# Order of the phases of sample attention in a decoder step: keys, values and what stands between them

## What is computed

```python
def nsa_heads(q, pos_q, comp, gather_sel, kv_win, pos_win, gates, slopes):
    o_c, p_c = cmp_attend(q, pos_q, comp, slopes)
    idx = select_blocks(jnp.sum(p_c, axis=3), pos_q, comp.shape[1])
    o_s = slc_attend(q, pos_q, gather_sel(idx), idx, slopes)
    o_w = win_attend(q, pos_q, kv_win, pos_win, slopes)
    o = (gates[:, :, 0, :, :, None] * o_c + gates[:, :, 1, :, :, None] * o_s
         + gates[:, :, 2, :, :, None] * o_w)
    return o.astype(q.dtype)
```

## Time and profile before

| | us |
|---|---|
| median of three runs | 905.23 (902.69 to 905.25) |
| the profiled execution, own time | 907.12 |
| its span | 905.3 |
| TensorE busy in the span | 828.0 |
| VectorE, ScalarE, GpSimd busy | 418.8, 336.5, 134.7 |
| sample attention, of the span | about 311.7 to 417.5 |

### The profile page before, as it was taken

How to read it: one execution, slowest core, us unless ns; L and a number is a source line. 1 busy time by engine, 2 the same in 40 slices (tenths; PEclk the granted TensorE clock), 3 DMA queues, 4 the chain that set the end, 5 groups by cost and what they waited for, 6 DMA issues and landing times.

```text
span 905.3 us, 18157 instructions
## 1 busy us (share of the span) xinstructions
PE 828.0 (91%) x7775; PEld 753.2 (83%) x7775; DVE 418.8 (46%) x782; ACT 336.5 (37%) x626; POOL 134.7 (15%) x160
## 2 busy tenths in 40 slices
PE   5999999886888867886999999999999999999995
PEld 4999977674555645565999999999999999999995
DVE  5435646665555475565327433344333433243432
ACT  6501155553466564454225431133212331043311
POOL 0001101100785345630220000000000000000120
PEclk9999999997899888886999999999999999999998
DMA  8922638832470206427221122222221122222002
GB/s 299 320 75 94 192 81 277 264 121 93 139 209 28 83 1 233 152 107 187 94 93 45 52 90 93 93 93 93 93 82 43 61 93 93 93 93 93 1 1 105
DMA packets 48793, 103.03 MB, mean 114 GB/s; under 512 B 7498, under 2 KB 19166, under 8 KB 46429
## 3 DMA queue, kind: packets, MB, share of 16 engines
q1 hardware_dynamic: 41821, 68.61, 23.0%
q0 software_dynamic: 6912, 33.56, 11.1%
HBM read 97.75 MB, written 8.53 MB: 117 GB/s over the span
## 4 chain that ended last, share of the span: by engine, by line
PE 52%; DVE 1%; ACT 0%; DVEq 0%; issue 0%
PE banks L2003 51%; PE banks L2044 0%; DVE y L1993 0%; PE banks L2070 0%; DVE wl L1923 0%; PE banks L2060 0%; ACT wh L1867 0%; DVE hT L1961 0%; DVE hT L1936 0%; DVE xl L1940 0%; ACT low L1881 0%; DVE xl L1929 0%; ACT xh L1883 0%; DVEq L1815 0%; ACT small L1911 0%
## 5 line engine op out<-in xcount | busy, mean ns | idle before, releaser
L2003 PE MATMUL banks<-xh,wh 128*128 128x288 f32 x640 | 138.2, 298 | 4.3 <-DVE xl L1929 3.9
L2003 PE MATMUL banks<-xh,wl 128*128 128x288 f32 x640 | 137.8, 297 | 0.0
L2003 PE MATMUL banks<-xl,wh 128*128 128x288 f32 x640 | 137.8, 297 | 0.0
L1867 ACT ACTIVATE wh<-low 128x1024 fp32r<-128x1024 f32 x72 | 75.2, 1052 | 103.0 <-PE banks L2003 102.7
L2003 PE MATMUL banks<-ah,wh 128*128 128x288 f32 x512 | 110.1, 297 | 0.0
L2003 PE MATMUL banks<-al,wh 128*128 128x288 f32 x512 | 109.7, 296 | 0.0
L2003 PE MATMUL banks<-ah,wl 128*128 128x288 f32 x512 | 109.7, 296 | 0.0
L2003 PEld LDWEIGHTS banks<-xh,wh 128*128 128x128 f32 x640 | 104.1, 190 | 5.0 <-DVE wl L1923 4.2
L2003 PEld LDWEIGHTS banks<-xl,wh 128*128 128x128 f32 x640 | 104.0, 190 | 0.0
L2003 PEld LDWEIGHTS banks<-xh,wl 128*128 128x128 f32 x640 | 103.9, 190 | 0.0
L1961 DVE TENSOR_TENSOR hT<-banks,hT 128x288 f32<-128x288 f32 x64 | 26.3, 453 | 138.9 <-PE banks L2003 138.9
(11 more groups left out here) (340 smaller groups left out, 1379.2 us busy)
## 6 DMA issues: line engine op xcount, KB each, us to landing
low<-in_w_up SPq DMA_DIRECT2D x8, 2048.0 KB, 8.3
low<-in_w_down SPq DMA_DIRECT2D x8, 2048.0 KB, 7.8
zone<-in_cmp_w SPq DMA_DIRECT2D x16, 256.0 KB
o_swin<-in_state_win SPq DMA_DIRECT2D x8, 504.0 KB
px<-in_x_prompt SPq DMA_DIRECT2D x4, 512.0 KB, 5.3
u_raw<-in_w_in SPq DMA_DIRECT2D x1, 2048.0 KB, 9.4
q_raw<-in_w_in SPq DMA_DIRECT2D x1, 2048.0 KB, 9.8
low<-in_state_win SPq DMA_DIRECT2D x4, 512.0 KB
```

Of the source, the lines that this page charges most:

```text
L1867: act.activation(wcols(m.wh, i), raw_cols(i), ACT.Copy).then_inc(wh_ready, 1)
L2003: last = pe.matmul(out(i, hf), w[wi], half(x[:, k, :], hf), start=first and part == 0, stop=end and part == 2)
```

## The change

The order becomes keys 0, keys 1, values 0, values 1, keys 2, keys 3, values 2, values 3: each engine's loop goes over two pairs b and b + 1. For odd pairs unit 3 is packed by ScalarE instead of VectorE, the compressed exponents stand at u = 5 instead of 1, and the importance matmul at i = 3 instead of 1. ScalarE runs `exponents(b)` between units 3 and 4 of the odd pair, copies all six probability blocks of an even pair and the first three of an odd one; VectorE copies the other three. GpSimd issues all pages of pairs 2 and 3 behind the additions of pair 1. The output of an even pair is turned within the values phase of the odd pair, that of pair 1 behind keys 2. The semaphore counts follow.

```diff
-    PACKER = ("act", "act", "act", "dve", "pool", "dve", "act", "pool", "dve", "act")
+    EVEN = ("act", "act", "act", "dve", "pool", "dve", "act", "pool", "dve", "act")
+    ODD = ("act", "act", "act", "act", "pool", "dve", "act", "pool", "dve", "act")
+    PACKER = [(EVEN, ODD)[n % 2] for n in range(NPAIR)]
...
+    COPIER = [(("act",) * VN, ("act",) * 3 + ("dve",) * 3)[n % 2] for n in range(NPAIR)]
...
+    def copied(n, i):
+
+        before = [COPIER[a][b] for a in range(NPAIR) for b in range(VN)][:VN * n + i + 1]
+        return pt_act if before[-1] == "act" else pt_dve, before.count(before[-1])
+
+    def keep_probs(eng, n, i):
+        copy = (lambda o, v: eng.activation(o, v, ACT.Copy)) if COPIER[n][i] == "act" else eng.tensor_copy
+        eng.wait_ge(p_turned, VN * n + i + 1)
+        if VN * n + i >= 3:
+            eng.wait_ge(v_done, VN * n + i - 2)
+        if i < X:
+            last = copy(m.spT[i % 3], pb[6 + i % 2][:, :])
+        else:
+            copy(m.spX[0:NS, 0:256], pb[6 + i % 2][0:NS, 0:256])
+            last = copy(m.spX[0:NBLK, 256:384], pb[6 + i % 2][0:NBLK, 256:384])
+        last.then_inc(copied(n, i)[0], 1)
...
-                if 1 <= n < NPAIR - 1:
-                    for i, x in enumerate(ORDER):
-                        if x < 4:
-                            pool.wait_ge(v_done, VN * (n - 1) + i + 1)
-                            for e in range(2):
-                                load_pages(pool, m, n + 1, e, x, sems)
+                if n == 1:
+                    for b in range(2):
+                        for i, x in enumerate(ORDER):
+                            if x < 4:
+                                pool.wait_ge(v_done, VN * b + i + 1)
+                                for e in range(2):
+                                    load_pages(pool, m, b + 2, e, x, sems)
...
-            for n in range(NPAIR + 1):
...
-                keep_output(n)
+            def keys_of(n, first, last):
+                for u in range(first, last):
+                    if u == (1, 5)[n % 2]:
+                        act.wait_ge(c_step, n * C_STEPS + 2)
+                        act.activation(m.sp[n % 2][:, CMP0:CMP0 + NBLK], m.sp[n % 2][:, CMP0:CMP0 + NBLK], ACT.Exp,
+                                       bias=cneg, accum_out=csum).then_inc(c_exp, 1)
+                    keep_keys(n, u)
+                    if u + 3 < UN and PACKER[n][u + 3] == "act":
+                        pack(act, n, u + 3)
+
+            for b in range(0, NPAIR, 2):
+                for u in range(3):
+                    pack(act, b, u)
+                keys_of(b, 0, UN)
+                if b:
+                    keep_output(b - 1)
+                for u in range(3):
+                    pack(act, b + 1, u)
+                keys_of(b + 1, 0, 4)
+                exponents(b)
+                keys_of(b + 1, 4, UN)
+                for i in range(VN):
+                    keep_probs(act, b, i)
+                exponents(b + 1)
+                for i in range(VN):
+                    if COPIER[b + 1][i] == "act":
+                        keep_probs(act, b + 1, i)
+                keep_output(b)
+            keep_output(NPAIR - 1)
...
-            for n in range(NPAIR + 1):
-                if n < NPAIR:
-                    small_scores(n)
+            def scores_of(n):
+                small_scores(n)
+                if PACKER[n][3] == "dve":
                     pack(dve, n, 3)
-                    compressed(n)
-                    pack(dve, n, 5)
...
-                    for i in range(3, VN):
...
-                    merge(n - 1)
+                compressed(n)
+                pack(dve, n, 5)
...
+
+            for b in range(0, NPAIR, 2):
+                scores_of(b)
+                scores_of(b + 1)
+                merge(b)
+                for i in range(VN):
+                    if COPIER[b + 1][i] == "dve":
+                        keep_probs(dve, b + 1, i)
+                merge(b + 1)
...
-                if n >= 3:
-                    pe.wait_ge(o_kept, n - 2)
+                if n >= 2:
+                    pe.wait_ge(o_kept, n - 1)
...
-                if n >= 2 and u < 2:
-                    pe.wait_ge(pt_dve, 3 * (n - 1))
+                if n == 2 and u < 2:
+                    pe.wait_ge(*copied(1, u + VN - 2))
...
                 if i == 0:
                     pe.wait_ge(exped, n + 1)
-                    pe.wait_ge(k_kept, UN * min(n + 2, NPAIR))
-                if i in (2, 3, 4):
-                    pe.wait_ge(pt_act, 3 * n + i - 1)
-                if i == 5:
-                    pe.wait_ge(pt_dve, 3 * n + 1)
+                    pe.wait_ge(k_kept, UN * (2 * (n // 2) + 2))
+                if i >= 2:
+                    pe.wait_ge(*copied(n, i - 2))
+                elif n % 2:
+                    pe.wait_ge(*copied(n - 1, i + VN - 2))
...
-                if i < 3:
-                    pe.wait_ge(pt_act, 3 * n + i + 1)
-                else:
-                    pe.wait_ge(pt_dve, 3 * n + i - 2)
+                pe.wait_ge(*copied(n, i))
                 if i == 0:
-                    pe.wait_ge(win_summed, min(n + 2, NPAIR))
+                    pe.wait_ge(win_summed, 2 * (n // 2) + 2)
                     if n:
                         pe.wait_ge(merged, n)
...
-            for n in range(NPAIR + 1):
...
+            def keys_of(n):
+                small_scores(n)
+                for i in range(X + 1):
+                    if i < X:
+                        turn_keys(n, 2 * i)
+                        turn_keys(n, 2 * i + 1)
+                    if i == (1, 3)[n % 2]:
+                        pe.wait_ge(p_cmp, n + 1)
+                        pe.matmul(pb[5][:, IMP:IMP + NBLK], const(m, "headsum"), m.sp[n % 2][:, CMP0:CMP0 + NBLK],
+                                  start=True, stop=True).then_inc(imp_mm, 1)
+                    if i in (2, 4, X):
+                        scores(n, TOGETHER[(i - 1) // 2])
+
+            def values_of(n):
+                for i in range(VN + 1):
+                    if i < VN:
+                        turn_probs(n, i)
+                    if i >= 1:
+                        values(n, i - 1)
+                    if i == 1 and n % 2:
+                        turn_output(n - 1)
+
+            for b in range(0, NPAIR, 2):
+                keys_of(b)
+                if b:
+                    pe.wait_ge(sel_step, b * SEL_STEPS + 1)
+                    turn_output(b - 1)
+                keys_of(b + 1)
+                values_of(b)
+                values_of(b + 1)
```

More of the change, by code:

```diff
@@ L1396, in pack @@
         x, e = ORDER[u // 2], u % 2
[L1397 removed]
+        if e == 0 or PACKER[n][u - 1] != PACKER[n][u]:
             if x < 4:
@@ L1405, in pack @@
         src = m.slot[2 * (n % 2) + e][:, x].rearrange("p q (g k) -> p q g k", g=NKV)[:, :, :, 0:HD]
[L1406 removed]
+        copy = (lambda o, v: eng.activation(o, v, ACT.Copy)) if PACKER[n][u] == "act" else eng.tensor_copy
         if u // 2 in SWAPPED:
             copy(dst[:, :, 0], src[:, :, 1])
[L1409 removed]
+            copy(dst[:, :, 1], src[:, :, 0]).then_inc(packed[PACKER[n][u]], 1)
         else:
[L1411 removed]
+            copy(dst, src).then_inc(packed[PACKER[n][u]], 1)
+    def copied(n, i):
[12 more added lines that the diff above has]
+        last.then_inc(copied(n, i)[0], 1)
     def count_packed(n, u):
[L1415 removed]
+        who = PACKER[n][u]
+        return sum(PACKER[a].count(who) for a in range(n)) + PACKER[n][:u + 1].count(who)
     with nc.Block() as block:
@@ L1510, in _ @@
-            for n in range(NPAIR - 2, NPAIR):
-                keep_output(n)
+            def keys_of(n, first, last):
[7 more added lines that the diff above has]
+                        pack(act, n, u + 3)
@@ new lines, in scores_of @@
+                compressed(n)
+                pack(dve, n, 5)
+                select(n)
+                dve.wait_ge(scored, X * n + 2)
+                dve.tensor_tensor_reduce(m.sp[n % 2][:, WIN0:WIN0 + WINDOW], bigconst(m, "s_win"), pb[4][:, :],
+                                         1.0, -3e38, ALU.add, ALU.max, mx(n)[:, 5:6]).then_inc(win_summed, 1)
+                for x in range(4):
+                    dve.wait_ge(pre_ready, n * 4 + x + 1)
+                    dve.wait_ge(scored, X * n + ORDER.index(x) + 1)
+                    a = 512 * x
+                    dve.tensor_tensor_reduce(m.sp[n % 2][:, a:a + 512], m.sp[n % 2][:, a:a + 512], pb[x][:, :],
+                                             1.0, -3e38, ALU.add, ALU.max, mx(n)[:, x:x + 1]).then_inc(summed, 1)
```

86 lines of the change are left out of this document (6 added, 80 removed).

## The result

The changed kernel takes 917.35 us (median of four runs, 916.43 to 919.89) against 905.24 for the kernel before beside it: a ratio of 1.013, 95% interval 1.010 to 1.016, so 12 us slower. The forecast was 915, range 905 to 923. Its profiled execution took 917.84 us with a span of 916.0.

The account below looks back on a forecast made before the run. TensorE's program order, waiting on steps other engines had not reached, was taken as the bound. Odd keys +8.9, values 0 -1.5, gap +1, values 1 +2.5, keys 2 -1, end 0 gave +9.9 us: median 915, range 905 to 923.

Parts of the forecast that it names:

- Keys 1: First odd keys phase: waits for unit 5's pack and pack 8 make it 21.9 us, 3.7 more than 18.2.
- Keys 3: Second odd keys phase, now directly behind a keys phase: 20.6 us (18.4 to 22.8) against 15.4, 5.2 more.
- its 1 us or so is covered: Start of keys 3: ScalarE's storing of pair 1's output costs nothing, since unit 5 comes 9 us into the phase.
- Values 0: Values phase of pair 0: later page issue hurts it less, 10.3 us, -1.5 (bounds -4.4 and 0).
- Gap ahead of values 1: TensorE ahead of values 1: exponents(b + 1), behind the sixth copy, end after TensorE's work, +1 us.
- values 1: Values phase of pair 1: page loads hurt it from its first matmul, 14.3 us, +2.5 (bounds -4.4 and +8.2).
- keys 2: Keys phase of pair 2: data early and most traffic over, -1 us, bound -2.9.
- Values 3: Last values phase: gap ahead absorbed by the 3.39 us gap ending a fixed time behind the w_out load, 0 (-2 to +1).
- rival 3: Values 0 and 1: gaps come of GpSimd's issue, not traffic, and both drop to 7.4 us: 899 us; 0.11 with rival 4.
- Rival 2: Odd keys phases: the clock stays up, both cost the lower bound (+4.5 together), 906 us in all; chance 0.14.
- rival 1: Values 1 meets the loads of both pairs throughout and takes 20 us, 921 us in all; chance 0.15.
- rival 4: Keys 1: pack 8 or compressed exponents bound nothing, so it comes to 14 to 15 us; 0.11 with rival 3.

Follow-up runs that it names:

- a5: Changed kernel with pack 5 of odd pairs ahead of the compressed step on VectorE: 914.25 us, ratio 1.009.
- a1: Changed kernel with pack 8 of odd pairs on ScalarE: 920.03 us, ratio 1.018.
- a3: Changed kernel without loading pages and windows of pairs 2 and 3: 908.16 us, ratio 1.004.
- c2: Changed kernel with pages of pairs 2 and 3 copied by SyncE, page numbers read from the real table into a register: 932.08 us, ratio 1.028.
- a8: a2 with odd pairs' compressed exponents ahead of exponents(b), copies split three and three, exponents(b + 1) behind the third: 908.70 us, ratio 1.005.
- b1: Kernel before without loading pages and windows of pairs 2 and 3: 888.46 us, ratio 0.982.
- b5: Kernel before with page loads of pairs 2 and 3 issued by SyncE as plain copies of as many bytes from other cache rows: 899.62 us, ratio 0.996.
- c1: Kernel before with pages of pairs 2 and 3 copied by SyncE, page numbers read from the real table into a register: 927.70 us, ratio 1.023.
- a2: Changed kernel with the new order alone, odd pairs keeping the old packers and old places of compressed exponents and importance matmul: 912.25 us, ratio 1.006.
- b3: Kernel before with the first half of w_out issued when all values are done: 909.3 us in one run.
- b7: Kernel before with 49 filler matmuls, 64 columns wide and never read, in the gap of keys 1: 906.46 us, ratio 1.003.
- b8: b7 with 24 fillers of 64 columns and 25 of 8: 910.66 us, ratio 1.006.

## Why the prediction was right, and where its steps were not

The direction, the place and the size came out: 917.4 against 915. That the total is so near is in part luck, as the steps show. By its own steps, with the bounds of the earlier trace rows:

- **Keys 1, 21.9 forecast.** Measured 23.1. Turn 5 came 10.3 us into the phase (9.9), the importance matmul 3.9 behind it, turn 8 another 3.45 behind (4.1 forecast), and the end 5.5 behind that, at the low clock (3.0 to 5.4 forecast). a5 shows the first wait to be the compressed step, and a1 the second to be pack 8, as the chain said. The term that was too small is the last, by 1.3 us: it ran at the low level, where I had half and half. My reading of the clock was also loose: in old keys 1 it is 0.62 from 330 to 333 us, which fits a fall near 330.7, behind the first gap and before the second.
- **Keys 3, 20.6.** Measured 22.5. The sum held the maxima of pair 2 4.1 us behind keys 2; they came at 4.7. The step that failed is "its 1 us or so is covered", said of the wait for the output, and of pack 3 "in ScalarE's free time". ScalarE in keys 3 of the changed kernel (timeline; the maxima were there at 389.4):

```profile
384.73 0.45 ACT L1490 ACTIVATE mixT<-banks 64x64 f32<-64x64 f32 x2 [1.51 <-PE banks L1712]
385.20 1.76 ACT L1409 ACTIVATE zone<-zone 128x512 f32<-128x512 f32 x4
...
389.99 0.71 ACT L1409 ACTIVATE zone<-zone 128x256 f32<-128x256 f32 x2
390.60 2.04 ACT L1499 ACTIVATE zone<-zone,small 128x2112 f32<-128x2112 f32 x1
```

  Storing the output delays the first packs, and pack 6 ends at 390.6, so the exponents start 1.2 us late and the gap is 5.19 instead of 4.38 us. Turn 5 thus came 10.4 us into the phase, where the sum had 8.6.
- **Values 0, -1.5.** Measured -0.3. The issue came 2.7 us behind the start of values 0, where I had 3.9, and the gaps and the late merge cost as before.
- **Gap ahead of values 1, +1; values 1, +2.5; keys 2, -1.** Measured 0.9, +1.7 and -0.7. The first two are right in size and not in kind, which is luck. The exponents of pair 1 did not wait for the maxima, there at 347.6, but for the sixth copy, and started at 353.5; where no loads stretch values 0, as in a3 and c2, the gap is 2.12 us. And values 1 did not grow by gaps through the whole phase: from 359.5 to 366 us TensorE has none, and its busy time rose by 2.7 us, with the clock at 0.67 instead of 1.00, while the idle time inside the phase fell by 1.0.
- **Values 3, 0.** Measured about +1. The step that failed is that the last gap "ends a fixed time behind the w_out load": it shrank to 1.67 us and ended not 10.8 us behind the w_out issue but 12.1 (425.84 against 413.76). Without the 2.12 us ahead of values 3 it is 10.8 to 11.0 us (before, a8, b1, b5, c1), with them 11.9 to 12.2 (a1, a2, a3, a5, c2 and the changed kernel), so 1.2 of the 2.12 us were not swallowed. The Trainium skill, "Runtime: NRT & Kernel Launch", section "Instruction fetch mechanics", calls the cost of crossing into the next block mostly hidden; the gap with its one instruction packet, b3 and b7 speak for one that is not.

The steps sum to +14.4 us of sample attention in the profiled execution against +9.9 forecast; the medians differ by 12.1. The sum was 4.5 us short, most of it in the two odd keys phases (3.1) and in values 0 (1.2), and the total is nearer than that.

Two premises were wrong though the sum was not hurt by them. First, the cost of the loads: I called it traffic. b5 and c2 show that it is not, so half of the premise of rival 3 was right: not the traffic. That it is the issue on GpSimd and not the kind of transfer isn't shown. Its outcome failed all the same, by the count of issues that stands against it in the prediction: 16 of them do not fit beside anything but the two values phases. The rule of the Trainium skill, "SBUF — State Buffer", section "Who interferes with whom", that DMA never contends with a compute engine, holds here for copies issued by SyncE (18.3 us with and 18.4 without traffic); beside GpSimd's indirect loads the same phases took 26.0 us. Second, I took the odd phases' length for the price of keys behind keys. a2 shows 16.1 us for such a phase with the old places of pack 3, exponents and importance. The later places cost 5 to 6 us a phase: unit 5 waits for its pack behind the late compressed step (3.3 and 4.1 us by a5), and unit 8 for the pack inside the selection with no TensorE work left to cover it. Had the change been the order alone, the same reasoning would have forecast too much.

Rival 2 fell on the clock (0.71 and 0.77 in the odd phases), rival 1 on values 1 (13.5 us, not 20), rival 4 on the gaps that a1 and a5 price.

## What to carry to other kernels

An importance or a selection step that is moved later takes its successors with it: before moving it, count the work that is left on the waiting engine behind it, and look for packs and copies that stand inside it in the other engine's list. A small step put ahead of a large one on the same engine gains nothing if the next hand-over waits behind the large one all the same (a8). Price a neighbour's phase by its cleanest instance (11.0 us here, with no loads) and not by one that already holds the losses the change will shift. A gap put down to "issue" can be a wait for another engine: look at what the others finished just before it. And if gaps lie beside transfers, change who issues them before calling them traffic.

## What the runs showed of the hardware that I had not expected

- While GpSimd issued eight indirect loads, TensorE idled on "issue" by mostly 0.2 to 0.5 us a time and a values phase took 4.4 us more (11.8 against 7.4); while SyncE's plain copies moved the same 4 MB in b5, values 0 took 7.4 us with no such gap. VectorE's merge came 2.3 us behind the end of the values in the kernel before, and 0.2 in b5.
- A copy whose row comes from a register took 0.8 us to issue on SyncE (24 in 19.11 us, c1); an indirect load of 512 KB took GpSimd 0.94 us and 0.30 behind it.
- Matmuls of 8 columns with a 128x128 fp32 weight took 0.12 us a record, those of 64 columns 0.13, both at the full clock (b8, 330 to 332 us).
- TensorE stood for 3.39 us until behind the one packet on the instruction queue, which came when w_out was nearly in; 98 matmul records more in its stream some 80 us earlier took the gap away (b7).
